# Attention softmax work cut into single-head pieces, with the router's key, flag and first one-hot table made ahead of the combination weights

## The reference, cut to what matters

```python
mixed = sigmoid(m_a) * (y_nsa @ w_proj_nsa) + sigmoid(m_b) * (y_gla @ w_proj_gla)
h = x + mixed @ w_out
# mixture of experts, 4 groups of 8 experts, 2 per token
combine = einsum('tk,tke->te', w, one_hot(expert_id))
for e in range(32):
    hdn = silu(v @ w_gate[e]) * (v @ w_up[e])
    y += (combine[:, e:e+1] * hdn) @ w_down[e]
```

## Time and profile before

| | |
|---|---|
| median of 3 runs | 1208.77 us (1208.45 to 1209.26) |
| the profiled execution | 1204.53 us, of which its span is 1202.7 us |
| PE busy | 1088.9 us, 91% of the span |
| DVE, ACT, POOL busy | 470.7, 411.8, 206.4 us |
| read from HBM | 331.32 MB, mean 276 GB/s |
| mean granted TensorE clock | 0.982 of full speed |

### The profile page before, as it was taken

How to read it: one execution, slowest core, us unless ns; L and a number is a source line. 1 busy time by engine, 2 the same in 40 slices (tenths; PEclk the granted TensorE clock), 3 DMA queues, 4 the chain that set the end, 5 groups by cost and what they waited for, 6 DMA issues and landing times. The chain is left out here.

```text
span 1202.7 us, 17403 instructions
## 1 busy us (share of the span) xinstructions
PE 1088.9 (91%) x6862; PEld 706.4 (59%) x6862; DVE 470.7 (39%) x1037; ACT 411.8 (34%) x786; POOL 206.4 (17%) x277
## 2 busy tenths in 40 slices
PE   8999888899898889788989899979999899999997
PEld 7887555557432324344545235346887676999775
DVE  4565366445200000133332112107747546344654
ACT  5444353343101001014332102004436454444872
POOL 1005363000000000002120000004422223001550
PEclk9999899999999999999999999999999999999998
DMA  9657399745799999999999999995531203766300
GB/s 364 233 173 259 126 350 351 266 175 226 286 425 426 422 426 415 424 427 401 418 428 422 422 423 421 424 419 205 172 128 53 89 21 121 223 182 190 107 20 35
DMA packets 55720, 333.58 MB, mean 277 GB/s; under 512 B 5840, under 2 KB 6096, under 8 KB 43216
## 3 DMA queue, kind: packets, MB, share of 16 engines
q1 hardware_dynamic: 55632, 332.39, 71.1%
HBM read 331.32 MB, written 1.05 MB: 276 GB/s over the span
## 5 line engine op out<-in xcount | busy, mean ns | idle before, releaser
L486 ACT ACTIVATE ab<-w 128x1024 fp32r<-128x1024 f32 (+2 forms) x117 | 122.0, 1049 | 178.9 <-PE ps L502 170.2
L496 DVE TENSOR_TENSOR ab<-w,ab 128x1024 fp32r<-128x1024 f32 (+2 forms) x96 | 116.8, 1223 | 133.4 <-ACT ab L486 133.0
L2548 PE MATMUL ps<-w,vT 128*32 128x512 f32 x1024 | 129.1, 629 | 41.2 <-DMA w<-in_w_gate 28.2
L502 PE MATMUL ps<-ab,uA 128*128 128x512 f32 x320 | 102.5, 402 | 5.8 <-POOL ab L496 2.6
L2548 PEld LDWEIGHTS ps<-w,vT 128*32 128x32 f32 x1024 | 29.1, 111 | 121.8 <-issue 79.7
L502 PE MATMUL ps<-UA,ab 128*128 128x256 f32 x512 | 93.8, 284 | 2.8 <-ACT h L1573 1.5
L502 PE MATMUL ps<-ab,UA 128*128 128x512 f32 (+1 forms) x288 | 87.9, 386 | 0.6 <-POOL UB L624 0.6
L502 PEld LDWEIGHTS ps<-UA,ab 128*128 128x128 f32 x512 | 80.2, 192 | 3.5 <-issue 1.7
L2596 PE MATMUL ps<-w,bT 128*32 128x512 f32 x512 | 62.0, 608 | 16.5 <-DMA w<-in_w_down 10.9
L502 PEld LDWEIGHTS ps<-ab,uA 128*128 128x128 f32 x320 | 60.5, 192 | 20.8 <-issue 3.4
L496 POOL TENSOR_TENSOR ab<-w,ab 128x1024 fp32r<-128x1024 f32 (+1 forms) x21 | 49.9, 2380 | 132.7 <-DVE Am L1804 88.1
(11 more groups left out here) (547 smaller groups left out, 1858.7 us busy)
## 6 DMA issues: line engine op xcount, KB each, us to landing
w<-in_w_gate SPq DMA_DIRECT2D x32, 2048.0 KB, 13.3
w<-in_w_up SPq DMA_DIRECT2D x32, 2048.0 KB, 12.9
w<-in_w_down SPq DMA_DIRECT2D x32, 2048.0 KB, 13.2
w<-in_w_ada SPq DMA_DIRECT2D x48, 512.0 KB, 7.6
w<-in_w_c SPq DMA_DIRECT2D x42, 512.0 KB, 4.5
w<-in_w_m SPq DMA_DIRECT2D x16, 512.0 KB, 5.3
w<-in_ab_out_w SPq DMA_DIRECT2D x10, 512.0 KB, 4.4
w<-in_w_out SPq DMA_DIRECT2D x8, 512.0 KB, 9.8
```

The source lines that it names most:

```text
L486: e.activation(sp.a(j), w.v, ACT.Copy).then_inc(sp.whole, 1)
L496: e.tensor_tensor(sp.b(j), w.v, sp.a(j).bitcast(F32), ALU.subtract).then_inc(sp.parts[j % NAB], 1)
L502: ins = e.matmul(out_, l[x], r[y], start=start and n == 0, stop=stop and n == 2)
L2548: ins = e.matmul(t.ps[o, :], ve[:, p % 2, 2 * c + k, o], w.v[:, 2 * a + k, :], start=c + k == 0, stop=c + k == 4)
```

## The change

- The attention work of DVE and ACT is emitted one head at a time, in slots of its own; `roots` moves from slot 0 to 2; `turned_out` ahead of `weighted`.
- Three slots of the level work are taken before the stage begins (`DECAY_AHEAD`), so POOL's and ACT's part of the first level is done there, and the level work runs three slots ahead of the modulations from then on.
- The first use of `pnsa0` (i = 0) moves into the attention stage, behind T(7).
- From c = 1 to `out1` the banks come from `UPPER`, six banks without 0 and 1. The first quarter of `cq` now stands between `mxT` and `out0`, in place of three filler matmuls, and holds banks 0 and 1 until `cq` is complete.
- The router's combination weights come after key, flag and the first one-hot table; the other three tables come after the first gather's copy.
- The context's first tiles are fetched once the `ogT` transposes are done, no longer once `pgla1` has read its weights, and the first of them stands ahead of the tiles of `out0` in SP's queue.

```diff
+        DECAY_AHEAD = 3
...
-            return nsa_steps([(0, 2, turn), (0, 0, scores), (5, 2, out)])
+            def behind(p):
+                if p == len(NSA_PAIRS) - 1:
+                    last()
+
+            return nsa_steps([(0, 2, turn), (0, 0, scores), (1, 2, behind), (5, 2, out)])
...
-            return nsa_steps([(2, 0, masked), (5, 1, weighted), (8, 2, turned_out)])
+            return nsa_steps([(1, 0, lambda p: masked(p, 0)), (2, 0, lambda p: masked(p, 1)), (6, 2, turned_out),
+                              (7, 1, lambda p: weighted(p, 0)), (9, 1, lambda p: weighted(p, 1))])
...
-            return nsa_steps([(1, 2, turned), (3, 0, weights)])
+            return nsa_steps([(1, 2, lambda p: turned(p, 0)), (2, 2, lambda p: turned(p, 1)),
+                              (3, 0, lambda p: weights(p, 0)), (6, 0, lambda p: weights(p, 1))])
...
-            return nsa_steps([(0, 1, roots)])
+            return nsa_steps([(2, 1, roots)])
...
+        UPPER = Ring(2, 3, 4, 5, 6, 7)
...
-            rest = turns(pe_modulations(e, ONE), pe_decayed(e, TWO))
-            beside(pe_nsa(e, FIVE), rest)
+            def project(n, x, p, c, i, ring=ALL):
+                ts, t = slice(i * 128, (i + 1) * 128), bank.take(ring, p + str(c))
+                free(e, t)
+                if c == 0:
+                    for y in bank[n] if n == "ogT" else bank[n][i::2]:
+                        e.wait_ge(y.evac, y.n)
+                for k in range(4):
+                    w = W[f"{p}{c}.{k // 2}"]
+                    if i == 0 and k % 2 == 0:
+                        e.wait_ge(w.full, w.n)
+                    ins = e.matmul(t.ps[:, :], x[:, k, ts], w.v[:, k % 2, :], start=k == 0, stop=k == 3)
+                ins.then_inc(t.full, 1)
...
+            decayed = pe_decayed(e, TWO)
+            for _ in range(DECAY_AHEAD):
+                next(decayed)
+            rest = turns(pe_modulations(e, ONE), decayed)
+            beside(pe_nsa(e, FIVE, lambda: project("nsa_o", ynT, "pnsa", 0, 0, FIVE)), rest)
...
-                    pe_lin(e, S1, "m11", uA, uB, 512, range(2))
+                    pe_lin(e, S1, "m11", uA, uB, 512, range(2), (), UPPER)
...
+                        if c + i > 0 or n == "ogT":
+                            project(n, x, p, c, i, UPPER if c == 1 else ALL)
+            pe_idle_next(e, UPPER, 4)
             e.wait_ge(mix_done, 4)
             for i in range(2):
-                pe_to_T(e, "mxT", lambda k: grow[:, i, :].rearrange("p (d k) -> p k d", k=8)[:, k, :], 8, ALL)
-            pe_idle_next(e, ALL, 3)
+                pe_to_T(e, "mxT", lambda k: grow[:, i, :].rearrange("p (d k) -> p k d", k=8)[:, k, :], 8, UPPER)
+            next(steps)
...
-                pe_to_T(e, "cnorm", lambda k: rows_c[i].rearrange("p (d k) -> p k d", k=8)[:, k, :], 8, ALL, (diag_ready, 1 + i))
+                pe_to_T(e, "cnorm", lambda k: rows_c[i].rearrange("p (d k) -> p k d", k=8)[:, k, :], 8, UPPER, (diag_ready, 1 + i))
...
+        def place_eight(e, x):
+            e.wait_ge(routing, KEYED)
+            for i in range(2):
+                ins = e.tensor_tensor(places_[:, i, x:x + 8, :], bc(C("iota")[:, 0:CAP], 1, 8), bc(key[:, i, x:x + 8], 2, CAP), ALU.is_equal)
+            ins.then_inc(placed, 1)
...
-            some(steps, 3)
+            some(steps, 2)
...
-            e.wait_ge(grp_exp, 1)
-            chain(e.tensor_reduce(sg[:, :, 0], eg, X, ALU.add))
             first_max(oh4, g4, m1, 4)
...
+            e.tensor_copy(flag[:, :], cnt[0:1, :]).then_inc(routing, 1)
+            place_eight(e, 0)
+            e.wait_ge(grp_exp, 1)
+            chain(e.tensor_reduce(sg[:, :, 0], eg, X, ALU.add))
...
             gathered(0)
+            for x in range(8, 32, 8):
+                place_eight(e, x)
...
-            if w.slot in EARLY_FOURS:
+            if w.slot in EARLY_FOURS or w.slot in CONTEXT and W.fresh[k]:
                 e.wait_ge(*use("ogT"))
-            elif w.slot in CONTEXT and W.fresh[k]:
-                e.wait_ge(*W.done["", "pgla1.1"])
```

More of the change, by code:

```diff
@@ L1313, in weights @@
-            def weights(p):
+                u, t = 2 * p + hp, bank["nsa_t"][2 * p + hp]
+                if u >= 3:
+                    g = bank["nsa_o"][(u - 3) // 2]
+                    e.wait_ge(g.full, g.n)
+                e.wait_ge(t.full, t.n)
+                e.activation(bT[:, u % 3, 0:n], t.ps[:, 0:n], ACT.Copy).then_inc(t.evac, 1)
+            def weights(p, hp):
                 i, m = NSA_PAIRS[p][1], st[:, p % 4, :]
                 n = 128 * (i + 1)
[L1316 to L1325, removed]
@@ L1327, in act_nsa @@
-            return nsa_steps([(1, 2, turned), (3, 0, weights)])
+                u, t = 2 * p + hp, bank["nsa_s"][2 * p + hp]
+                e.wait_ge(t.evac, t.n)
+                if u >= 4:
+                    g = bank["nsa_t"][u - 4]
+                    e.wait_ge(g.full, g.n)
+                for kind in range(2):
+                    o, c = slice(kind * n, kind * n + n), 2 * hp + kind
+                    ins = e.activation(NSA_P[u % 4][:, o], bS[:, hp, o], ACT.Exp, bias=m[:, c:c + 1], scale=-1.0, accum_out=m[:, 4 + c:5 + c])
@@ L1564, in pe_first @@
             for c in range(2):
-                pe_lin(e, S1, f"out{c}", uA, uB, 512, range(2))
+                pe_lin(e, S1, f"out{c}", uA, uB, 512, range(2), (), UPPER)
         def act_evac(e, name, outs, f=ACT.Copy, scaled=False):
@@ L1661, in act_first @@
                     act_splits(e, S1, "m01.3")
+            decayed = act_decayed(e)
+            for _ in range(DECAY_AHEAD):
+                next(decayed)
             act_lin(e, S1, "m01", [xsm[:, i, 0, :] for i in range(2)], more=0, scaled=True)
-            rest = turns(act_modulations(e), act_decayed(e))
+            rest = turns(act_modulations(e), decayed)
             beside(act_nsa(e), rest)
@@ L1856, in dve_first @@
             dve_lin(e, S1, "m01", more=0)
-            rest = turns(dve_modulations(e), dve_decayed(e))
+            decayed = dve_decayed(e)
+            for _ in range(DECAY_AHEAD):
+                next(decayed)
+            rest = turns(dve_modulations(e), decayed)
             beside(dve_nsa(e), rest)
@@ L1926, in pool_first @@
                 e.tensor_tensor(st[:, 2 + i, :], st[:, 2 + i, :], gate[:, i, 0:24:3], ALU.mult).then_inc(c_rec, 1)
-            beside(pool_nsa(e), turns(idle_modulations(), pool_decayed(e)))
+            decayed = pool_decayed(e)
+            for _ in range(DECAY_AHEAD):
+                next(decayed)
+            beside(pool_nsa(e), turns(idle_modulations(), decayed))
             pool_rsqrt(e, 2, 2, (squared, 2))
@@ L3405, in _ @@
         def _(e):
-            pe_first(e)
-            W.ring, W.context = Ring(*range(12)), Ring(*CONTEXT)
-            pe_route(e, pe_context_a(e))
+            W.context = Ring(*CONTEXT)
+            steps = pe_context_a(e)
+            pe_first(e, steps)
+            W.ring = Ring(*range(12))
+            pe_route(e, steps)
             marks.append(len(W.order))
```

90 lines of the change are left out of this document (33 added, 57 removed).

## The result

The changed kernel takes 1220.74 us (median of 6 runs, 1218.00 to 1223.31) beside 1209.29 of the kernel before (6 runs, 1208.45 to 1213.81): ratio 1.0090, 95% interval 1.0066 to 1.0113. So it is slower, as forecast, but by 11.5 us where 6.2 were summed up, and it lies above the range. Timed once more it is 1219.57 (6 runs) against 1209.93, ratio 1.0081 (1.0060 to 1.0101).

What follows compares the result with a forecast made beforehand. The prediction took the expert stage as bound by its 2 MB tile stream, which PE's path starts. Its terms, -0.4 + 1.7 + 0.3 + 4.1 + 1.7 + 1.0 - 2.2 = +6.2 us, put on the median, gave 1215.0 us, range 1206 to 1219.

Steps and rivals of the forecast that it cites:

- Attention stage, order: Attention stage: walking the new order of each engine's work gave a net gain of 0.4 us.
- the stops at the end: End of the attention stage: PE stands 2.6 us before the last modulation, then 1.35 and 2.7 us around T(7).
- Clock at its end: End of the attention stage: the stops bring one stretch of half clock, +1.7 us, bounds 0 and 3.4.
- The third rival: Two slow-clock losses at each place, attention end and bank wait: 1218.4 us, or 1220 with upper bounds; chance 0.15.
- Banks: Second half of `pgla0` waits for DVE, +0.3; `pgla1` stops about 4.7 us between halves, +4.1, with slow clock behind, +1.7.
- The cq tile: Transfers: the first `cq` tile ahead of the `out0` tiles delays ACT and so `cnorm`, +1.0 us, bounds 0 and 1.4.
- The moved quarter and the reorder: From `mxT` to the experts: `out0` starts 0.6 later, the router stage loses 2.9; -2.2 us with hand-overs, bounds -2.6 and 0.

Runs made afterwards that it cites:

- e1: The changed kernel with all banks but those of `mxT` and the output projection taken from all eight again; 1212.46 us, ratio 1.0027 to the kernel before.
- e6: The kernel before with only the single-head attention pieces and the decay work 3 steps ahead; 1216.53 us, ratio 1.0073 to the kernel before.
- e10: The kernel before with single-head attention pieces and decay work 3 steps ahead, but both heads' `weighted` in one slot; 1215.89 us, ratio 1.0043.
- e3: The changed kernel with ten idle matmuls in the hole between the halves of `pgla1`; 1216.37 us, ratio 1.0068 to the kernel before.
- e2: The kernel before with only the six-bank ring added, from `m11` to `out1`; 1214.47 us, ratio 1.0041 to the kernel before.
- e4: The changed kernel with both `weighted` in slot 7 and the moved projection half ahead of T(7), from another ring; 1214.54 us, ratio 1.0058.
- e8: The changed kernel with the first `cq` tile fetched just before the `out1.0` tile; median 1216.31 us, ratio 1.0062 to the kernel before.
- e9: The kernel before with the `cq` quarter moved, its tile fetched late and six banks for `mxT` and the output projection; 1207.60 us, ratio 0.9979.
- e7: The kernel before with only the router's reorder; 1210.01 us, ratio 1.0010 to the kernel before.
- e5: The changed kernel with the edits of e1, e4 and e8 together; 1206.90 us, ratio 0.9978 to the kernel before.

## Why the prediction was right in its sign and too low in its size

**Attention stage, order (-0.4).** The places and sizes of the stops at the end were right to 0.15 us. The sum was 1.3 too low: the first column grows by 3.6, of which 2.7 is slow clock at its end (1.09 for 0.60 and 5.88 for 3.67), so the order costs +0.9, with the slow clock of the start taken back as forecast (2.6 of waits less 1.7). With the starts of the stage put level, S(7) came 0.7 later than walked and T(7) 1.1; the rest gathers behind it in steps of 0.1 to 0.2.

**Clock at its end (+1.7).** This is the step that failed, here and behind the bank wait. It counted one loss of a size read from one stretch. The two profiles of the changed kernel show 2.7 and 4.2 at the end of the stage, and the second has 1.7 more in its middle; e1 4.3, e6 5.3, e10 4.8, but e3, with the same stops, 1.5. So the same stops cost one to three such losses, and one profile doesn't tell how many. The third rival, two losses at each place, named this and had 0.15.

**Banks (+0.3, +4.1, +1.7).** The first is +0.4. The second is shown by e1, e2 and e3: the stop is 4.66, and without the clock the column is 3.9 longer. The clock was mis-sized again: 2.8 and 2.7 in the two profiles of the changed kernel, 2.9 in e4, 2.4 in e2, 1.8 in e8. The Trainium skill's rule ("TensorE: Matmul & The Clock Gate", "HAM oscillation") that long holes put PE back to half its clock is borne out by e3, where the same time filled with idle matmuls left the clock at 1.00.

**The cq tile (+1.0).** `cnorm` waits 1.39 instead of 0.47; the column has +0.9 in the first profiles, +0.8 in the second ones, and e8 takes back 1.3. Right in size; the profile names no releaser for that wait, so the way over ACT is not shown.

**The moved quarter and the reorder (-2.2).** At full clock 45.49 against 47.94: -2.45. Right as a sum, and the reason given is borne out: the counts' one-hot sum is just in time because the wait for ACT now stands behind it. In e9, which lacks the reorder, DVE still waits 1.47 for ACT and PE 1.51 for the sum. Whether key, flag and first table ahead of the combination weights are worth anything was in no run of its own; e7 shows only that the whole reorder gains nothing while the quarter is where it was.

**The sum.** In place of +6.2 the columns give 3.6 + 0.4 + 0.9 + 6.7 - 2.45 = +9.2 in the first profile and 6.7 + 0.4 + 0.8 + 6.5 - 2.45 = +12.0 in the second; the medians differ by 11.5 and 9.6. Of the missing 3.0 us in the first profile 2.1 are slow clock and 1.3 the order; of the 5.8 in the second 5.2 are slow clock and 1.2 the order; the other terms take 0.4 to 0.6 back.

**Open.** The third slow stretch, between the logits and the counts, to which the prediction gave nothing, cost 3.4 in both profiles of the changed kernel, 0 and 1.7 in those of the kernel before; but 0 in e8 and e3, which are the changed kernel at this place, and 3.4 in e2, e6 and e10, which are the kernel before at this place. The others have 3.4 (e1, e4), 1.7 (e5), 0 (e7) and 1.7, behind the counts, in e9. It comes and goes in one program, and PE is hardly idle ahead of it (4.89 of 5.00 us busy from 300 to 305, 5.00 of 5.00 from 305 on). How much of the difference of the medians comes from its falling more often, one or two profiles for each kernel can't say. Slow clock also falls where nothing was edited: e9's first column is 1.7 longer than that of the kernel before, with the same attention stage. And 8.8 us for e6 is 2.3 more than its first column; its profile has the third stretch too (3.4), but with one profile each it is not shown where the median's 2.3 are.

**The version to keep.** e5 and e9 are both faster than the kernel before by 0.2%, near the limit of what this measurement tells, and faster than the changed kernel by 1%. The moved quarter and the reorder in the kernel before, without the attention pieces, were not tried together; nor was the earlier first level alone, which in all nine traces that have it leaves no slow clock at the start of the stage (1.7 us lost there in the five without it).

## What to carry to other kernels

A stop of 2.7 us or more on TensorE's path in the stages compared here cost its own length and, unless the hole was filled, another 1.5 to 3.7 us in slow matmuls behind it; where several stops stood close together the slow matmuls cost 1.5 to 5.3 us from profile to profile. Price both, take more than one profile, and don't take the one loss that the trace of before happens to hold. When part of a ring of banks is reserved for one user, count where the others now come around to: the wait lands on the consumer that empties its bank last in its own queue. If a hole can't be closed, put long matmuls into it that are due anyway (e5) or that do nothing (e3); and when one edit shortens a chain and another what waits for it, each alone may be worth little.

## What the runs showed of the hardware that was not expected

TensorE went to its lower level with almost no idle time ahead: the windows 305:310 and 310:315 of the changed kernel have PE busy for 5.00 of 5.00 at 0.78 and 0.54. Just before, PE did 16 transposes and 32 matmuls of 36 columns. The Trainium skill ("TensorE: Matmul & The Clock Gate", "Part 4: PE-mode transpose") says that transposes do not count as activity in the same way; the trace agrees in direction, but the same work kept 1.00 in four other profiles (the first of before, e3, e7, e8), so it can't be the only condition. Within one program the execution time goes in part with the mean granted clock: over the 80 executions of the kernel before that were timed beside the experiments, with clocks from 0.975 to 0.988, the correlation with the time is -0.66, and 0.001 less clock goes with 0.6 us more.
